# Four spread products of a pair's first expert, moved to a place among its second expert's products

## The chip, the cores and the metric

One Trainium2 chip, one core of it. The metric is the device time of one execution in microseconds (us), taken as the median of the runs. The core has a matrix engine (PE in the profile, with its weight loads listed as PEld), a vector engine (DVE), an activation engine (ACT), GpSimd (POOL), and a queue processor (SP) that here only issues loads. All data is float32; each matrix product stands in the trace as two PE records.

## The reference

Two layers of a diffusion backbone run on two groups of 128 tokens of width 1024 that share one set of weights. Each layer has a token mixer and then a mixture of experts, which is the part that matters here:

```python
def hier_moe(h, w_rg_l, w_re_l, w_e1_l, w_e3_l, w_e2_l):
    x = h.reshape(-1, D_)
    ...
    gate = jnp.einsum('nk,nke->ne', w_top, jax.nn.one_hot(expert_id, N_EXPERTS, dtype=f32))
    hid = jax.nn.silu(jnp.einsum('nd,edf->nef', x, w_e1_l)) * jnp.einsum('nd,edf->nef', x, w_e3_l)
    y = jnp.einsum('nef,efd->nd', hid * gate.astype(x.dtype)[..., None], w_e2_l)
```

There are 16 experts; each token goes to two of them. An expert has three weight matrices: w1 and w3 of 1024 x 512 and w2 of 512 x 1024, 2 MB each.

## The kernel before

A layer first runs its token mixer (a stream of weight chunks against both groups' tokens) and its output projection, router and ranking. Then come the experts, in a pass over all 16 with room for 64 tokens in each; more passes would run only if an expert had more than 64 tokens, and none does here. What is computed for one expert, with `e` its number:

- gather (`gather`, L1021): the tokens routed to the expert are picked out of `h2tok` by products with a 0/1 matrix `e_pick`. One gather serves a pair of experts (64 columns each) and comes in two parts of 8 products. Each part is copied out of PSUM bank XG by DVE (L1723) into `xgT`; the second part waits for the copy of the first, since both use that bank. `e_pick` for the next pair is made by DVE (`pick_pair`, L1709), after it has finished the silu of the pair's second expert.
- two up projections (`up`, L1035), with w1 (`up(0, ...)`) and w3 (`up(1, ...)`), 16 products each. After `up(0)`, ACT and DVE work out the sigmoid and silu (L1310, L1728 to L1730); after `up(1)`, DVE multiplies the two (L1737, `ehid`).
- transposes: of the selection matrix `e_sel` (L1055) and of the hidden values (L1062); ACT copies both out of PSUM (L1318 `e_selT`, L1320 `ehidT`).
- down projection (L1074), 8 products, into PSUM bank OUT; ACT copies it out (L1323, `e_out`).
- spread (`spread_group`, L1042): four products that put the expert's 64 result rows back on the two groups' tokens and add them up in PSUM over all experts.

PE runs experts in pairs (`pair(p, e)`, `i` 0 and 1, eight pairs to a layer) in an order written out by hand. For a pair (a, b) in the middle of the pass it is: up(1) of a; transpose of e_sel; two spreads of the expert before a; transposes of the hidden values; its two other spreads; down of a; up(0) of b; four spreads of a; up(1) of b; gather part 0 for the next pair; transposes of b; gather part 1; down of b; up(0) of the next pair's a. The last pair has no gathers. `n` numbers the expert steps from 1, and each semaphore counts one per step (spread counts four), with one step given in advance.

The weights of the experts come through `ring`, three slots of 2 MB: w1, w3 and w2 of the current expert have one slot each. SP issues the load of a slot for the next expert as soon as PE has finished the last product that reads it; that wait and that issue are all SP does in this stage, in this order and for each expert in turn:

```python
sp.wait_ge(slot_used, used_e(l, p, e, free))
sp.dma_start(ring[:, r, :], dram["stream"][...]).then_inc(slot_loaded[r], 16)
```

For the first expert of a layer w1 and w3 are loaded elsewhere in advance, so its ring slots already hold the second expert's.

Of the kernel before, what the change touches and what calls it, by code (L numbers as in the profile page):

```python
# [36 lines left out]
G = 2  # L37
# [153 lines left out]
def build(nc, dram, out):  # L191
    ctx = ExitStack()
    with ctx:
# [3 lines left out]
        def sem(name):  # L197
            return ctx.enter_context(nc.semaphore(name))
# [126 lines left out]
        def bank(b, n=1):  # L325
            return psum[:, b, :] if n == 1 else psum[:, b:b + n, :]
# [123 lines left out]
        selT_ready = sem("selT_ready")  # L450
# [52 lines left out]
        def ring_e(l, j):  # L503

            return (RING_BASE[l] + FIRST_EXPERT[l] - AHEAD + j) % RING

        def arrived_e(l, p, e, j):

            return p * (NE * 16) + e * 16 + ((RING_BASE[l] + FIRST_EXPERT[l] - AHEAD + j) // RING + 1) * 16

        def step(l, p, e):

            return l * STEPS + p * NE + (e + 1)
# [169 lines left out]
        def _(pe):  # L683
# [68 lines left out]
            for l in range(DEPTH):  # L752
# [150 lines left out]
                for q in ([0, 2, 1, 3] if l == 0 else [0, 1, 2, 3]) + list(range(4, QUARTERS)):  # L903
                    c, g, part = q // 4, (q // 2) % 2, q % 2
# [110 lines left out]
                def gather(n, part, at):  # L1015

                    pe.wait_ge(pick_ready, n + 2)
                    pe.wait_ge(xg_ready, n + part if at == XG else n)
                    for j in range(4):
                        for g in range(G):  # L1020
                            mm = pe.matmul(psum[:, at, j * P:(j + 1) * P], h2tok[:, g, (4 * part + j) * P:(4 * part + j + 1) * P],  # L1021
                                           e_pick[:, g, :], start=(g == 0), stop=(g == G - 1))
                    mm.then_inc(gathered, 1)

                def up(j, p, e, i, ahead=False):

                    if ahead:
                        pe.wait_ge(ahead_loaded[j], l * 16 + 16)
                        w_up = ahead_slot[j].rearrange("p (k n) -> p k n", k=KT)
                    else:  # L1030
                        pe.wait_ge(slot_loaded[ring_e(l, j)], arrived_e(l, p, e + i, j))
                        w_up = ring[:, ring_e(l, j), :].rearrange("p (k n) -> p k n", k=KT)
                    for k in range(KT):
                        for hf in range(2):
                            mm = pe.matmul(psum[halves_of[hf], UP[j], 0:FE // 2], xgT[:, k, halves_of[i]], w_up[:, k, hf * (FE // 2):(hf + 1) * (FE // 2)],  # L1035
                                           start=(k == 0), stop=(k == KT - 1))
                    mm.then_inc(slot_used, 1)

                def spread_group(n, i, g, opens=False, closes=False):

                    for hf in range(2):
                        pe.matmul(bank(Y_MOE[g][hf]), e_selT[i][halves_of[hf], g, :], e_out[halves_of[hf], :], start=opens, stop=closes)\  # L1042
                          .then_inc(spread, 1)

                def pair(p, e, first=False, last=False):
                    for i in range(2):
                        n = step(l, p, e + i)
                        up(1, p, e, i, ahead=first and i == 0 and isinstance(p, int))
                        if i == 1 and not last:
                            gather(n + 1, 0, XG)  # L1050

                        pe.wait_ge(sel_ready, n + 1)
                        pe.wait_ge(eout_ready, n)
                        for g in range(G):
                            mm = pe.transpose(psum[:, OUT, g * P:(g + 1) * P], e_sel[:, g, :], ident)  # L1055
                        mm.then_inc(sel_turned, 1)
                        if i == 0 and not first:
                            pe.wait_ge(selT_ready, n)
                            spread_group(n - 1, 1, 0)
                        pe.wait_ge(hid_ready, n + 1)  # L1060
                        for j in range(2):
                            mm = pe.transpose(psum[:, UP[0], j * P:(j + 1) * P], ehid[:, j * P:(j + 1) * P], ident)  # L1062
                        mm.then_inc(hid_turned, 1)
                        if i == 0 and not first:
                            spread_group(n - 1, 1, 1)
                        if i == 1 and not last:
                            gather(n + 1, 1, XG)

                        pe.wait_ge(hidT_ready, n + 1)
                        pe.wait_ge(selT_ready, n + 1)  # L1070
                        pe.wait_ge(slot_loaded[ring_e(l, 2)], arrived_e(l, p, e + i, 2))
                        for k in range(BT):
                            for hf in range(2):
                                mm = pe.matmul(psum[halves_of[hf], OUT, :], ehidT[:, (k % 2) * P + (k // 2) * CAP:(k % 2) * P + (k // 2) * CAP + CAP],  # L1074
                                               w_down[:, k, hf * W:(hf + 1) * W], start=(k == 0), stop=(k == BT - 1))
                        mm.then_inc(slot_used, 1)
                        if i == 0:
                            up(0, p, e, 1)
                        elif not last:
                            pe.wait_ge(xg_ready, n + 3)  # L1080
                            up(0, p, e + 2, 0)
                        if i == 0 or last:
                            pe.wait_ge(eout_ready, n + 1)
                            for g in range(G):
                                spread_group(n, i, g, opens=first and i == 0, closes=last and i == 1)

                def expert_pass(p):
                    n = step(l, p, 0)
                    pe.wait_ge(eout_ready, n)
                    gather(n, 0, XG)  # L1090
                    gather(n, 1, OUT)
                    pe.wait_ge(xg_ready, n + 2)
                    up(0, p, 0, 0, ahead=isinstance(p, int))
                    pair(p, 0, first=True)
                    with pe.Fori(2, NE - 3, 2) as e:
                        pair(p, e)
                    n_fullest = fullest_expert(pe, l) if isinstance(p, int) else None
                    pair(p, NE - 2, last=True)
                    return n_fullest
# [927 lines left out]
```

## Time and profile before

| | |
|---|---|
| median of 3 runs | 1465.44 us (1465.32 to 1470.59) |
| the profiled execution, its own time | 1467.44 us |
| its span in the profile | 1465.7 us |
| PE busy | 1380.3 us, 94% of the span |
| DVE busy | 520.5 us, 36% |
| ACT busy | 233.9 us, 16% |
| DMA | 259 GB/s over the span, 379.92 MB |

The span is the time from the first to the last instruction of the profile; 1.7 us of the execution lie around it, and the median is 2.0 us under the profiled execution's time. The profile lists, by engine, when each instruction ran, how long the engine sat idle before it, and what released it. The starts of matrix products are exact to some 10 ns and their ends are modelled, so the text below takes times between starts. "x16" behind a row is its number of records, so it is eight products. The experts' stage runs from about 484 to 738 us in layer 0, and from about 1194 to 1447 us in layer 1.

### The profile page before, as it was taken

Reading aid. Unit: us, or ns where it says so; the run is one execution under the profiler, and the core shown is the slowest. Engines: PE = TensorE matmul, PEld = TensorE weight load, DVE = VectorE, ACT = ScalarE, POOL = GpSimd, SP = SyncE. Lnnn points to the kernel's source line nnn. Section 1 sums busy time; section 2 is a strip of 40 time slices with the busy share of each in tenths; the row PEclk is TensorE's granted clock in tenths of the full one; section 3 lists DMA queues with packets and bytes.
Section 4 is the critical chain, followed back from the end, with each engine's and each line's share of the span. In section 5 each row is a group of like instructions: output and inputs, shape, how many; then the busy total and the mean of one; then the engine's idle time right before and its main releaser. Section 6 shows DMA issues by size and latency. Waiting matters only on the chain. (4 is left out here: it accounts for less than half of the span.)

```text
span 1465.7 us, 16950 instructions
## 1 busy us (share of the span) xinstructions
PE 1380.3 (94%) x6662; PEld 723.2 (49%) x6662; DVE 520.5 (36%) x984; ACT 233.9 (16%) x436; POOL 151.1 (10%) x130
## 2 busy tenths in 40 slices
PE   6999989989999999999979999999999999999994
PEld 2445445444445555555534554554444465555551
DVE  1353444422134422323244443452412452322324
ACT  0131220222201011111112122112221111111110
POOL 0123150021200000000001222501120000000000
PEclk9999999999999999999999999999999999999997
DMA  9754544645458299999874445344446628999992
GB/s 384 307 229 157 203 180 143 243 180 223 183 197 331 99 396 396 413 414 412 334 288 174 182 153 200 138 186 186 186 151 234 277 94 332 414 413 397 410 414 113
DMA packets 40263, 379.92 MB, mean 259 GB/s; under 512 B 7946, under 2 KB 12170, under 8 KB 17292
## 3 DMA queue, kind: packets, MB, share of 16 engines
q1 hardware_dynamic: 31776, 375.83, 63.8%
q10 hardware_dynamic: 8428, 3.29, 0.8%
q8 instruction: 39, 0.64, 0.2%
q14 instruction: 20, 0.16, 0.0%
HBM read 374.76 MB, written 4.33 MB: 259 GB/s over the span
## 5 line engine op out<-in xcount | busy, mean ns | idle before, releaser
L926 PE MATMUL psum<-ring,hT 128*128 128x512 f32 x1152 | 520.1, 600 | 13.7 <-DVE rows L1598 8.1
L926 PEld LDWEIGHTS psum<-ring,hT 128*128 128x128 f32 x1152 | 213.8, 192 | 255.1 <-issue 247.5
L1035 PE MATMUL psum<-ring,tbuf 128*64 128x256 f32 x1920 | 216.0, 380 | 1.2 <-DMA ring<-in_stream 1.2
L1035 PEld LDWEIGHTS psum<-ring,tbuf 128*64 128x64 f32 x1920 | 136.0, 137 | 94.2 <-issue 17.5
L1074 PE MATMUL psum<-ring,tbuf 128*64 128x512 f32 x512 | 116.9, 598 | 1.9 <-ACT tbuf L1320 1.9
L1592 DVE TENSOR_TENSOR ch<-psum,bias_ring 128x512 f32<-128x512 f32 x68 | 46.8, 689 | 166.3 <-PE psum L926 166.3
L1728 DVE TENSOR_SCALAR tbuf<-tbuf 128x256 f32<-128x256 f32 x32 | 9.4, 294 | 247.7 <-ACT tbuf L1310 247.7
L950 PE MATMUL psum<-ring,tbuf 128*128 128x512 f32 x192 | 82.9, 593 | 0.0
L1021 PE MATMUL psum<-tbuf,ch 128*128 128x128 f32 x512 | 68.3, 290 | 7.7 <-DVE tbuf L1723 5.0
L1878 POOL TENSOR_SCALAR ldata<-ldata 128x512 f32<-128x512 f32 x24 | 46.1, 1920 | 280.8 <-ACT ldata L1272 269.3
L1021 PEld LDWEIGHTS psum<-tbuf,ch 128*128 128x128 f32 x512 | 62.7, 200 | 16.5 <-issue 9.5
L1827 POOL TENSOR_TENSOR tbuf<-const,sm 128x512 f32<-128x512 f32 x16 | 20.8, 1321 | 480.4 <-DVE sm L1474 453.5
L1042 PE MATMUL psum<-tbuf 64*128 64x512 f32 x256 | 67.4, 626 | 1.4 <-ACT tbuf L1323 1.4
L1074 PEld LDWEIGHTS psum<-ring,tbuf 128*64 128x64 f32 x512 | 33.9, 136 | 70.0 <-issue 59.4
L950 PEld LDWEIGHTS psum<-ring,tbuf 128*128 128x128 f32 x192 | 36.3, 190 | 45.1 <-issue 45.0
L964 PE MATMUL psum<-ring,hT 128*128 128x512 f32 x128 | 55.8, 594 | 1.4 <-ACT hT L1282 1.4
L1729 DVE RECIPROCAL tbuf<-tbuf 128x256 f32<-128x256 f32 x32 | 56.1, 1753 | 1.1
L347 POOL TENSOR_TENSOR hbuf<-hbuf 128x512 f32<-128x512 f32 x28 | 44.0, 1572 | 80.5 <-PE psum L772 80.5
L772 PEld LDWEIGHTS psum<-hbuf 128*128 128x128 f32 x256 | 34.9, 196 | 24.7 <-issue 13.8
L1323 ACT ACTIVATE tbuf<-psum 128x512 f32<-128x512 f32 x32 | 19.1, 597 | 154.6 <-PE psum L1074 154.6
L347 DVE TENSOR_TENSOR hbuf<-hbuf 128x512 f32<-128x512 f32 x28 | 21.6, 770 | 61.9 <-PE psum L772 61.9
L772 PE MATMUL psum<-hbuf 128*128 128x128 f32 x256 | 37.9, 293 | 5.8 <-ACT hbuf L1156 5.6
(269 smaller groups left out, 1153.6 us busy)
## 6 DMA issues: line engine op xcount, KB each, us to landing
ring<-in_stream SPq DMA_DIRECT2D x158, 2048.0 KB, 9.3
ch<-in_stream SPq DMA_DIRECT2D x6, 2048.0 KB, 12.3
bias_ring<-in_b_in SPq DMA_DIRECT2D x36, 256.0 KB, 8.2
ldata<-in_ldata SPq DMA_DIRECT2D x2, 2329.0 KB, 23.7
hbuf<-in_ln SPq DMA_DIRECT2D x4, 1024.0 KB, 11.8
hbuf<-in_stream SPq DMA_DIRECT2D x1, 2048.0 KB, 8.1
tbuf<-in_stream SPq DMA_DIRECT2D x1, 2048.0 KB, 11.6
ch<-in_lb_logits SPq DMA_DIRECT2D x2, 1024.0 KB, 13.4
```

The costliest lines, as they stand in the source:

```text
L347: return engine.tensor_tensor(v, v, other.unsqueeze(3).to_broadcast([P, 2, W // (2 * half), half]), ALU.mult)
L772: mm = pe.matmul(psum[:, PP, hp], (k_x if i else k_sum)[:, hp], crossing(Q_B, Q_F, 1 << (i - 1), hp) if i else q_T[:, hp], start=True, sto ...
L926: mm = pe.matmul(bank(PJ + g), hT[:, k, g * P:(g + 1) * P], w[:, k, :], start=(k == 0), stop=(k == KT - 1))
L950: mm = pe.matmul(bank(BR_BANK[g] + hf), brT[:, b % 2, k, g * P:(g + 1) * P], w[:, k, hf * W:(hf + 1) * W], start=(k == 0), stop=(k == BT - 1))
L964: mm = pe.matmul(bank(2 * hf + g), hT[:, k, g * P:(g + 1) * P], w[:, k, :], start=(k == 0), stop=(k == KT - 1))
L1021: mm = pe.matmul(psum[:, at, j * P:(j + 1) * P], h2tok[:, g, (4 * part + j) * P:(4 * part + j + 1) * P], e_pick[:, g, :], start=(g == 0), ...
L1035: mm = pe.matmul(psum[halves_of[hf], UP[j], 0:FE // 2], xgT[:, k, halves_of[i]], w_up[:, k, hf * (FE // 2):(hf + 1) * (FE // 2)], start=(k ...
L1042: pe.matmul(bank(Y_MOE[g][hf]), e_selT[i][halves_of[hf], g, :], e_out[halves_of[hf], :], start=opens, stop=closes)\
L1074: mm = pe.matmul(psum[halves_of[hf], OUT, :], ehidT[:, (k % 2) * P + (k // 2) * CAP:(k % 2) * P + (k // 2) * CAP + CAP], w_down[:, k, hf * ...
L1592: ins = tt(ch[:, g, c if c < 12 else GATE_BUF[c - 12], :], bank(PJ + g), bias_ring[:, c % RING, :], ALU.add)
L1729: mlink(dve.reciprocal(esig, esig))
L1878: pool.tensor_scalar(sig, sig, 1.0, LN_MAX, ALU.add, ALU.min).then_inc(sig_plus, 1)
```

## The change

The four spread products of the pair's first expert (`i == 0`) no longer stand behind up(0) of the second. They are issued in the second expert's turn, behind its transposes and ahead of gather part 1 (in the last pair: ahead of the down projection, as there is no gather). The products are the same. A wait for `selT_ready` stands before them; the waits for `eout_ready` that covered them are those for the transposes of the same turn. The spreads of each pair's second expert stay where they were, and so do the last pair's four at the very end.

```diff
@@ in pair(p, e, first, last), for i in range(2)
                         mm.then_inc(hid_turned, 1)
                         if i == 0 and not first:
                             spread_group(n - 1, 1, 1)
+                        if i == 1:
+                            pe.wait_ge(selT_ready, n)
+                            for g in range(G):
+                                spread_group(n - 1, 0, g, opens=first)
                         if i == 1 and not last:
                             gather(n + 1, 1, XG)
...
                         elif not last:
                             pe.wait_ge(xg_ready, n + 3)
                             up(0, p, e + 2, 0)
-                        if i == 0 or last:
+                        if i == 1 and last:
                             pe.wait_ge(eout_ready, n + 1)
                             for g in range(G):
-                                spread_group(n, i, g, opens=first and i == 0, closes=last and i == 1)
+                                spread_group(n, 1, g, closes=True)
```

## Rows read from the trace of the kernel before

**Rows 1.** The page's second part: DMA busy tenths in 40 slices of 36.6 us

```profile
DMA  9754544645458299999874445344446628999992
```

**Rows 2.** Windows: us long; busy us (instructions) by engine; clock, DMA share, GB/s

```profile
core 0: us, PE busy (x) PEld busy (x) DVE busy (x) ACT busy (x) POOL busy (x), PEclk, DMA share, GB/s
481.00:485.00 4.00, 2.65 (x18) 2.10 (x17) 1.92 (x12) 0.20 (x1) 0.00 (x0) 1.00 0.00 0
485.00:489.00 4.00, 4.00 (x23) 4.00 (x22) 1.87 (x8) 0.00 (x0) 0.00 (x0) 0.57 0.02 4
656.00:687.00 31.00, 30.65 (x220) 17.15 (x218) 9.02 (x18) 3.39 (x8) 0.00 (x0) 1.00 0.98 410
718.00:719.00 1.00, 0.04 (x2) 0.00 (x0) 0.00 (x0) 0.60 (x1) 0.00 (x0) 1.00 1.03 442
```

**Rows 3.** Timeline of PE, sixth pair of layer 0: start us, length, line, operation, records

```profile
656.43 3.62 PE L1035 MATMUL psum<-ring,tbuf 128*64 128x256 f32 x32
659.98 1.99 PE L1042 MATMUL psum<-tbuf 64*128 64x512 f32 x8
661.90 3.67 PE L1035 MATMUL psum<-ring,tbuf 128*64 128x256 f32 x32
665.50 2.05 PE L1021 MATMUL psum<-tbuf,ch 128*128 128x128 f32 x16
667.39 0.38 PE L1055 MATMUL psum<-const,tbuf 128*128 128x128 f32 x2
667.61 0.38 PE L1062 MATMUL psum<-const,tbuf 128*128 128x128 f32 x2
668.34 2.05 PE L1021 MATMUL psum<-tbuf,ch 128*128 128x128 f32 x16 [0.35 <-DVE tbuf L1723]
670.32 3.65 PE L1074 MATMUL psum<-ring,tbuf 128*64 128x512 f32 x16
673.80 7.08 PE L1035 MATMUL psum<-ring,tbuf 128*64 128x256 f32 x64
...
682.24 0.44 PE L1062 MATMUL psum<-const,tbuf 128*128 128x128 f32 x2
682.61 1.13 PE L1042 MATMUL psum<-tbuf 64*128 64x512 f32 x4
```

**Rows 4.** Timeline of SP's queue: three load issues around that pair

```profile
643.43 0.33 SPq L650 DMA_DIRECT2D ring<-in_stream  x1
...
650.35 0.33 SPq L650 DMA_DIRECT2D ring<-in_stream  x1
...
674.16 0.33 SPq L650 DMA_DIRECT2D ring<-in_stream  x1
```

**Rows 5.** DMA view (last column us to landing), issues at 502.9, 582.0, 643.4, 650.4, 711.8

```profile
ring<-in_stream SPq DMA_DIRECT2D x1, 2048.0 KB, 7.5
...
ring<-in_stream SPq DMA_DIRECT2D x1, 2048.0 KB, 8.1
...
ring<-in_stream SPq DMA_DIRECT2D x1, 2048.0 KB, 7.7
...
ring<-in_stream SPq DMA_DIRECT2D x1, 2048.0 KB, 10.6
...
ring<-in_stream SPq DMA_DIRECT2D x1, 2048.0 KB, 12.1
```

**Rows 6.** Timeline of DVE, same pair

```profile
663.21 0.74 DVE L1709 TENSOR_SCALAR tbuf<-const,tbuf 128x64 f32<-128x64 f32 x4 [0.16 <-DVE tbuf L1730]
...
667.59 0.69 DVE L1723 COPY tbuf<-psum 128x512 f32<-128x512 f32 x1 [1.55 <-PE psum L1021]
```

**Rows 7.** Timeline of PE, last pair of layer 0

```profile
724.54 3.67 PE L1035 MATMUL psum<-ring,tbuf 128*64 128x256 f32 x32
...
728.79 0.44 PE L1062 MATMUL psum<-const,tbuf 128*128 128x128 f32 x2 [0.21 <-SPq L669]
729.70 3.65 PE L1074 MATMUL psum<-ring,tbuf 128*64 128x512 f32 x16 [0.47 <-ACT tbuf L1320]
```

## The prediction

> **What bounds the kernel now.** I read the profile in four steps. First, where the change acts: only in the experts' stage, where the DMA line of the page stands at 9 for slices 15 to 19, counted from 1 [rows 1]. Second, the windows of that stage. In 31 us of it PE is busy 30.65 us at the full clock, and the DMA engines have a share of 0.98 [rows 2]. So two resources look full, and the busy shares can't say which one sets the pace. Third, the timeline of PE through one pair, to see what each product waits for. The only stall it names is 0.35 us in front of gather part 1, waiting for DVE's copy of part 0 [rows 3]. Fourth, the loads. A ring slot is loaded again only when PE has finished with it, so a late product delays a load, and a late load delays a product one expert later. That loop has to be followed through both engines.
>
> The pair of [rows 3] has the period of its neighbours: from the end of one second expert's down projection, seen in the issue of its load at 643.43, to the next at 674.16 is 30.73 us [rows 4]. The load issued at 643.43 finds an empty DMA queue, because the products before it took long and released nothing. It lands 7.7 us later [rows 5]. The two loads issued behind it queue up; the second, w3 for this pair's second expert, is issued at 650.35 and lands 10.6 us later, at 660.95 [rows 4, 5]. That is 17.5 us after the first issue. The up projection that reads it starts at 661.90 [rows 3]. So today the weights are there 0.95 us before they are wanted, and what PE does in between is part of the four spreads that the change takes away from this place.
>
> **What leaves.** The spreads take 661.90 - 659.98 = 1.92 us between the two up projections [rows 3]. Without them up(1) of the second expert could start 3.46 us after up(0) (two up projections back to back have a length of 7.08, one has 3.62 [rows 3]), instead of 5.47 us after. That would be 2.0 us earlier, but the weights land at 660.95, so it starts 0.95 us earlier and PE stands idle for about 1.0 us. The cover that the spreads gave to a load is gone, and half of the time won goes into waiting for it. From a slot's landing to the first product I add 0.05 us, an estimate; its bounds are 0 and 0.3, the latter from the 0.35 us that the gather waits in all for its copy [rows 3].
>
> **What comes.** In the second expert's turn the transposes of the hidden values are now followed by eight PE records of spreads. Before, from that transpose to gather part 1 it took 668.34 - 667.61 = 0.73 us, with the stall for DVE's copy in it. Where a spread follows that transpose today, it takes 682.61 - 682.24 = 0.37 us. So the new stretch is 0.37 + 1.92 = 2.29 us, 1.56 us more than before [rows 3]. The copy that the gather waited for starts at 667.59 and takes 0.69 us [rows 6], so it ends inside the spreads; that stall is gone, and it is the one real gain, about 0.36 us. The added wait for `selT_ready` costs nothing: that copy was made a whole expert earlier, before a down projection that has long finished. Behind it on PE stand the spreads, gather part 1 and the down projection; nobody but they wait on it. The other engines issue the same instructions. ACT's wait for spreads in front of its copy of bank OUT comes after a down projection that itself stands behind the moved spreads. On SP nothing is moved, but each issue follows PE's releases: w1 and w3 for the next pair come earlier, w2, behind the down projection, comes later.
>
> **The sum for a pair in the middle.** I follow the loop from the issue of w2's load (behind the down projection of a second expert) to its next issue: 17.5 us to the landing of w3 [rows 4, 5]; 0.05 to its first product; 3.60 for up(1) (661.90 to 665.50); 1.89 for gather part 0; 0.22 from one transpose to the other; 0.37 + 1.92 for transpose and spreads; 1.98 for gather part 1 (668.34 to 670.32); 3.48 for the down projection (670.32 to 673.80) [rows 3]; 0.36 from there to the issue at 674.16 [rows 4]. That is 31.37 us against 30.73 now: 0.64 us more for a pair. The same view from PE alone: 0.9 us gained at up(1), 1.56 us lost behind the transposes. The time goes into the DMA engines: six loads keep them busy and the seventh, lone one is issued later, so their pause in each pair grows.
>
> **First and last pair.** In a layer's first pair every weight is there in time, but another wait comes next. The gather needs `e_pick`, and DVE finishes it at 663.21 + 0.74 = 663.95, which is 7.52 us after up(0) began at 656.43 [rows 3, 6]. PE would reach the gather 3.46 + 3.60 = 7.06 us after it. So the gather starts 9.07 - 7.52 = 1.55 us earlier than now and the spreads cost 1.56 behind it: nothing is left. In the last pair w3's load, issued at 711.8, lands 12.1 us later, at 723.9; up(1) starts at 724.54 [rows 5, 7], so 0.6 is gained. From the hidden transposes to the down projection it is 729.70 - 728.79 = 0.91 us [rows 7] and will be 2.29, 1.38 more, so 0.75 us lost in sum. A layer has six middle pairs: 6 x 0.64 + 0.75 = 4.6 us. Two layers, and nothing between them that could take it up, since the layer norm and the next layer's work wait for the last spread: 9.2 us. On the profiled execution's 1467.4 us that gives 1476.6. The median of the runs lies 2.0 us below it, so I predict 1474.7 us.
>
> **Bounds.** The uncertain term is the landing of a lone load, on which the two queued ones stand. The lone loads in the stage took 7.5 to 8.1 us, with 7.7 in the pair that I used [rows 5]. The change makes the queue emptier at that point, so I stay with 7.7 and take the ends for the range: from -0.2 to +0.4 us in each of 12 pairs, that is 6.8 to 14.0 us. The forecast's own range is 1472.2 to 1479.4.
>
> **Rivals.** (1) No change. If the lone load landed about 1 us sooner, w3 would be there in time. Then the wait for `e_pick` would be the bound in every pair as in the first, the middle pairs would give nothing, and only the last pair's up(1), 1.9 us earlier against 1.38, would bring 0.5 us in a layer: 1464.4 us. Against it stand all the loads shown, none under 7.5 us [rows 5]; for it, that DMA engines with less to do might serve a lone load sooner. Chance 0.14. The Trainium skill would put us here: its page "DMA: Bandwidth & Descriptors", section "Anatomy of one DMA", gives a fixed 2.0 us plus the bytes over 436 GB/s, an estimate of 6.8 us for such a load, and by it the loop above would be 30.5 us, less than today's 30.73. The trace disagrees by 0.9 us, and the measurement decides.
>
> (2) Faster. The same, and `e_pick` ends 0.47 us sooner because DVE's chain gets shorter. Then PE alone sets the pace and gains 0.44 us in each of 12 pairs and 0.5 in each last one: 1459 us. Nothing in the change shortens that chain of DVE, so 0.04.
>
> (3) Slower by much more. The granted clock falls after PE's idle time: ahead of 485 us PE was busy only 2.65 of 4 us, and in the next 4 us the mean clock was 0.57, nearly all of it at the lower level of 1.2 GHz [rows 2]. Were that to happen behind every new wait, it would cost up to some 1.7 us (half of the 3.4 us that the 0.57 stands for) in 12 pairs, and give about 1495 us. It decides from an idle time longer than the one at 718 us, where PE did nothing for 0.97 us and the clock stayed at 1.00 [rows 2]; the new wait is as long as that one. Chance 0.05.
>
> (4) The spreads don't move in effect, for instance because their stretch is swallowed by another wait in the second expert's turn: 1465.4 us, 0.02; the timeline shows no wait of 1.9 us there.
>
> The same page of the Trainium skill advises, in "Rules for kernel authors", to issue a load early, compute, and wait late. The change does the opposite for w3: it takes computing from ahead of the wait. The trace agrees so far as it shows the landing 0.95 us before the start.
>
> **How the numbers follow.** The forecast has 0.75, rivals (1) to (4) have 0.14, 0.04, 0.05 and 0.02. A measurement of this kernel can tell about 0.5% from no change, which is 7.3 us, so the forecast counts as slower only above 1472.8; its own range reaches just under that, and I put 0.58 of its 0.75 above and 0.17 below. Slower is 0.58 + 0.05 = 0.63; the same is 0.17 + 0.14 + 0.02 = 0.33; faster 0.04. The range takes in rival (1) and the forecast's ends: 1464 to 1479.
>
> **What would show it.** In the changed kernel's timeline up(1) of a middle pair's second expert should have an idle time of about 1 us before it, ended by the DMA of the ring, and start 17.5 us after the lone load's issue. From the transposes to gather part 1 there should be 2.3 us, with no stall for the copy. The period from one lone load to the next should be 31.4 us, the DMA share a little lower, and the gather part 0 should wait for `e_pick` in the first pair alone. A period of 30.7 with a stall at gather part 0 would speak for (1), one of 30.3 for (2), a clock below 1.00 in the stage for (3). The prediction is wrong if lone loads land sooner than 7.5 us, or if the eight records of the moved spreads cost less than 1.9 us in their new place.

## The result, and the profile after

| | before | changed |
|---|---|---|
| median of the runs | 1465.38 us (1464.4 to 1470.59) | 1475.44 us (1471.83 to 1478.86) |
| ratio, 95% interval | | 1.0062 [1.0044, 1.0079] |
| span of the profiled execution | 1465.7 us | 1477.1 us |
| PE busy | 1380.3 us | 1379.1 us |
| mean DMA rate over the span | 259 GB/s | 257 GB/s |
| layer 0's experts | 244.8 us | 248.3 us |
| layer 1's experts | 244.2 us | 249.1 us |

The kernel is slower by 10.1 us in the medians; the forecast was 9.2 (1474.7 us), in a range of 1464 to 1479. The two last lines of the table are worked out from the timeline of PE, from the start of the first up projection of a layer to the start of its last spread record: that is the stretch that the change can alter, called the stage below. They grew by 3.4 and 4.9 us, 8.4 in all. The other 3.0 us by which the two spans differ stand ahead of layer 0's experts, where no instruction differs (the first up projection starts at 493.62 in place of 490.62). So some of the closeness of 10.1 to 9.2 is chance, and the test of the mechanism is in the stages.

The timeline of PE for the sixth pair of layer 0, the pair that [rows 3] shows of before (start us, length, line, records, idle time before it and what ended it):

```profile
661.47 3.62 PE L1035 MATMUL psum<-ring,tbuf 128*64 128x256 f32 x32
666.06 3.67 PE L1035 MATMUL psum<-ring,tbuf 128*64 128x256 f32 x32 [0.96 <-DMA ring<-in_stream]
669.66 2.05 PE L1021 MATMUL psum<-tbuf,ch 128*128 128x128 f32 x16
671.55 0.38 PE L1055 MATMUL psum<-const,tbuf 128*128 128x128 f32 x2
671.77 0.38 PE L1062 MATMUL psum<-const,tbuf 128*128 128x128 f32 x2
672.08 1.99 PE L1042 MATMUL psum<-tbuf 64*128 64x512 f32 x8
674.00 2.05 PE L1021 MATMUL psum<-tbuf,ch 128*128 128x128 f32 x16
675.98 3.65 PE L1078 MATMUL psum<-ring,tbuf 128*64 128x512 f32 x16
679.46 7.08 PE L1035 MATMUL psum<-ring,tbuf 128*64 128x256 f32 x64
```

The spreads have left the place behind the first row, and in their stead stands an idle time of 0.96 us, ended by the DMA of the ring. Behind the transposes the eight records of the spreads stand now, and the 0.35 us stall ahead of gather part 1 is gone.

The queue of SP around that pair, and from the DMA view the time to landing of the first two of these issues:

```profile
648.48 0.33 SPq L650 DMA_DIRECT2D ring<-in_stream  x1
...
655.39 0.33 SPq L650 DMA_DIRECT2D ring<-in_stream  x1
...
679.82 0.33 SPq L650 DMA_DIRECT2D ring<-in_stream  x1
```

```profile
ring<-in_stream SPq DMA_DIRECT2D x1, 2048.0 KB, 7.8
...
ring<-in_stream SPq DMA_DIRECT2D x1, 2048.0 KB, 10.6
```

The lone load (w2's) is issued at 648.48. w3's load is issued at 655.39 and lands 10.6 us later, at 666.0, 17.5 us after the lone load's issue, and up(1) starts at 666.06. From one lone load's issue to the next it is 679.82 - 648.48 = 31.34 us, where before it was 30.73 [rows 4]. The window of a pair, with the fields of [rows 2], and the group of all up projections in layer 0's stage (busy us, mean ns of one | idle us before them, and what ended it):

```profile
656.00:687.00 31.00, 30.04 (x218) 16.88 (x216) 8.69 (x18) 3.08 (x8) 0.00 (x0) 1.00 0.96 401
```

```profile
L1035 PE MATMUL psum<-ring,tbuf 128*64 128x256 f32 x960 | 107.7, 380 | 7.2 <-DMA ring<-in_stream 6.0 <-SPq L669 1.2
```

PE is busy 30.04 us of the 31 where it was busy 30.65, the DMA share is 0.96 for 0.98, the rate 401 GB/s for 410, and the clock is still 1.00 [rows 2]. PE and the DMA engines both looked full, and both have become less full: that is what a longer loop looks like.

### The profile page after: what moved, and what is told of

Its sections match the earlier page's. It is cut to its first block and busy times, and to the rows that moved or that the text cites. A ratio compares the mean times of both kernels' runs of the same rounds, so it can differ in the third digit from the quotient of the medians.

```text
span 1477.1 us, 16950 instructions
## 1 busy us (share of the span) xinstructions
PE 1379.1 (93%) x6662; PEld 721.7 (49%) x6662; DVE 520.3 (35%) x984; ACT 234.0 (16%) x436; POOL 151.1 (10%) x130
## 5 line engine op out<-in xcount | busy, mean ns | idle before, releaser
L926 PEld LDWEIGHTS psum<-ring,hT 128*128 128x128 f32 x1152 | 214.3, 193 | 257.8 <-issue 248.3
L1035 PEld LDWEIGHTS psum<-ring,tbuf 128*64 128x64 f32 x1920 | 136.3, 137 | 102.5 <-DMA ring<-in_stream 24.6
L1727 DVE COPY tbuf<-psum 128x512 f32<-128x512 f32 x32 | 22.1, 691 | 68.5 <-PE psum L1021 68.5
## 6 DMA issues: line engine op xcount, KB each, us to landing
tbuf<-in_stream SPq DMA_DIRECT2D x1, 2048.0 KB, 11.7
```

The source lines that it names most:

```text
L926: mm = pe.matmul(bank(PJ + g), hT[:, k, g * P:(g + 1) * P], w[:, k, :], start=(k == 0), stop=(k == KT - 1))
```

## The experiments

With each version the kernel before ran on the same chip; the times below are medians, the ratios those to the kernel before. Experiments 1 and 2 edit the kernel before, and so does the first half of experiment 3; the others edit the changed kernel. "A pair's period" is the time from one second expert's down projection to the next one's. Two theories were to be told apart. The load loop: the loss arises because w2's load is issued later, and because up(1) can't use the time won, its weights not being there. Its rivals: the new place costs time by itself, whatever the loads do, or PE and DVE alone set the pace.

**1. The old place alone.** The first experts' spreads are left out of the middle pairs.

```diff
                         if i == 0 or last:
                             pe.wait_ge(eout_ready, n + 1)
-                            for g in range(G):
-                                spread_group(n, i, g, opens=first and i == 0, closes=last and i == 1)
+                            if i == 0 and not first and not last:
+                                pe.sem_inc(spread, 2 * G)
+                            else:
+                                for g in range(G):
+                                    spread_group(n, i, g, opens=first and i == 0, closes=last and i == 1)
```

> The kernel before, with the four spreads of a pair's first expert left out of the six middle pairs of each layer (that part of the experts' sum is not computed); first and last pair as before. It tests the half of the sum that says what leaving the old place is worth. Theory of the load loop: up(1) of the second expert can't start before w3 has landed, 17.5 us after the lone load's issue, so only about 0.9 us of the 1.92 are won in a middle pair: period 29.8 us, an idle time of 1.0 us before that up(1) ended by the DMA, and 12 x 0.9 = 11 us in all, about 1454.5 us. Rival, PE and DVE alone set the pace: the next bound is e_pick, 1.5 us are won in each, period 29.2 us, about 1447.5 us.

Measured: 1455.69 us beside 1466.39, ratio 0.9905 [0.9871, 0.9939], 10.7 us less. The timeline of PE in a middle pair:

```profile
628.52 3.62 PE L1035 MATMUL psum<-ring,tbuf 128*64 128x256 f32 x32
632.94 3.67 PE L1035 MATMUL psum<-ring,tbuf 128*64 128x256 f32 x32 [0.80 <-DMA ring<-in_stream]
```

It waits for the DMA, and the period (from the down projection at 611.69 to that at 641.37) is 29.7 us, not 29.2. So of 1.92 us of work taken away 1.0 is won in this pair, and 0.8 in the mean of the twelve (two of them have a period of 30.5 and 31.0 us); the loads hold the rest. The stages are 5.5 and 4.5 us shorter.

**2. The new place alone.** Nothing is taken away; four more products stand where the change puts the spreads.

```diff
+                        if i == 1:
+                            for g in range(G):
+                                for hf in range(2):
+                                    pe.matmul(bank(UP[1]), e_selT[0][halves_of[0], g, :], e_out[halves_of[0], :], start=True, stop=True)
                         if i == 1 and not last:
                             gather(n + 1, 1, XG)
```

> The kernel before, with its spreads where they were, and four products of the same size more (into a PSUM bank whose content is no longer wanted) in the place to which the change moves the spreads, in all pairs. It tests the other half of the sum, what the new place costs. Theory: 2.29 us in place of 0.73 between the transposes and gather part 1, the stall for DVE's copy gone, so 1.56 us more in seven pairs of a layer and 1.38 in the last; the period becomes 32.3 us, PE's own chain being longer then than the load loop, and up(1) of the second expert doesn't wait. About 24.6 us more, 1490 us. Rival, that the new place is cheap because DVE's copy and ACT's copies are waited for anyway: less than 1 us for a pair, under 1480 us.

Measured: 1516.43 us beside 1466.39, ratio 1.0326 [1.0280, 1.0373], twice the loss that I expected. The products themselves were not what I had taken them for:

```profile
582.94 0.38 PE L1062 MATMUL psum<-const,tbuf 128*128 128x128 f32 x2
583.25 3.70 PE L1069 MATMUL psum<-tbuf 64*128 64x512 f32 x8
586.87 2.05 PE L1021 MATMUL psum<-tbuf,ch 128*128 128x128 f32 x16
```

Eight records take 3.70 us here; the eight of the spreads take 1.99 [rows 3]. With 3.62 us from start to start in place of 1.92, the 1.70 us more make 27 us in 16 pairs, and the miss is of that size. The run doesn't measure the new place, so it was made again with two products.

```diff
+                        if i == 1:
+                            for g in range(G):
+                                pe.matmul(bank(UP[1]), e_selT[0][halves_of[0], g, :], e_out[halves_of[0], :], start=True, stop=True)
```

> The run with four extra products measured 3.70 us for them where the four spreads take 1.99: its products all read the first 64 rows, while a spread's two halves read rows 0 to 63 and 64 to 127 and run side by side. So here only two extra products, one after the other, which should take as long as four spreads: a length of about 1.9 us in the new place. Otherwise as before: the kernel before, nothing taken away. Theory: 1.56 us more in seven pairs of a layer and 1.38 in the last, period 32.3 us, 24.6 us in all, about 1491 us. Rival, that part of the extra cost in the run with four was something else than the length of the products: over 1495 us.

Measured: 1486.59 us beside 1466.46, ratio 1.0133 [1.0104, 1.0162]; the two stages are 11.5 and 11.3 us longer, 22.8 in all for 24.6 expected (the medians differ by 20.1). The place costs nearly what was reckoned:

```profile
579.79 0.38 PE L1062 MATMUL psum<-const,tbuf 128*128 128x128 f32 x2
580.10 1.98 PE L1068 MATMUL psum<-tbuf 64*128 64x512 f32 x4
582.01 2.05 PE L1021 MATMUL psum<-tbuf,ch 128*128 128x128 f32 x16
583.99 3.65 PE L1077 MATMUL psum<-ring,tbuf 128*64 128x512 f32 x16
```

From the transposes to gather part 1 it is 582.01 - 579.79 = 2.22 us in place of 0.73, and the period is 32.2 us (583.99 to 616.21). That is 1.5 us more a pair, so the rival that the place is cheap falls. The forecast had 1.56; the difference comes from the step between transposes and products, 0.31 us where I took 0.37. The changed kernel shows the same 0.31.

**3. Short loads.** Both kernels with half of each ring load of the experts. The other half of each slot keeps older values, so the results are others.

```diff
-                    sp.dma_start(ring[:, r, :], dram["stream"][e * 3 + (l * SLOTS + FIRST_EXPERT_SLOT + j)])
+                    sp.dma_start(ring[:, r, 0:SLOT // 2], dram["stream"][e * 3 + (l * SLOTS + FIRST_EXPERT_SLOT + j), :, 0:SLOT // 2])
```

> The kernel before with only half of each ring load of the experts' weights (1 MB in place of 2 MB; the other half of the slot keeps older values, so the experts' results are others). Loads can't set the pace here. Theory: PE's own chain remains, with a period of 30.7 us as before; only the few waits for a slot go, about 1 to 3 us in all, so about 1463 us. Rival, that the loads already set the pace before the change: a period clearly under 30.7 us, and 10 us or more faster.

> The changed kernel with the same half loads. Theory of the load loop: the loss of the change is gone with the loads. up(1) starts right behind up(0), gather part 0 waits about 0.4 us for e_pick, nothing is left over in the middle pairs (period 30.7 us) and the last pair wins 0.6 us, so within 2 us of the kernel before with half loads (1462 us or so). Rival, that the new place costs more whatever the loads do, for instance through the copies of ACT and DVE: 8 to 10 us slower than that kernel, a period of 31.3 us.

Measured: the kernel before with half loads 1462.14 us, ratio 0.9964 [0.9948, 0.9981]; the changed kernel with half loads 1460.32 us, ratio 0.9954 [0.9927, 0.9981]. The stages last 243.6 us (both layers) and 243.2 us. So with loads this short nothing of the change's loss is left; before the change the loads cost only 1.2 and 0.6 us in a stage. The kernel before keeps its period with half loads, so before the change the pace of a middle pair was PE's own chain:

```profile
610.31 3.65 PE L1074 MATMUL psum<-ring,tbuf 128*64 128x512 f32 x16
...
641.03 3.65 PE L1074 MATMUL psum<-ring,tbuf 128*64 128x512 f32 x16
```

That is 30.72 us from start to start. In the changed kernel with half loads the period is 30.80, and the next wait is the one for `e_pick`:

```profile
564.15 7.08 PE L1035 MATMUL psum<-ring,tbuf 128*64 128x256 f32 x64
571.81 2.05 PE L1021 MATMUL psum<-tbuf,ch 128*128 128x128 f32 x16 [0.58 <-DVE tbuf L1713]
```

**4. Only the lone load shortened**, in the changed kernel.

```diff
-                    sp.dma_start(ring[:, r, :], dram["stream"][e * 3 + (...)]).then_inc(slot_loaded[r], 16)
+                    if j == 2:
+                        sp.dma_start(ring[:, r, 0:SLOT // 2], dram["stream"][e * 3 + (...), :, 0:SLOT // 2]).then_inc(slot_loaded[r], 16)
+                    else:
+                        sp.dma_start(ring[:, r, :], dram["stream"][e * 3 + (...)]).then_inc(slot_loaded[r], 16)
```

> The changed kernel, with only the w2 loads halved (1 MB; the other half of that slot keeps older values, so the down projections compute with wrong weights there); w1 and w3 are loaded whole. In a middle pair the lone load is that of w2, and w1 and w3 queue behind it. Theory: the lone load lands 2.4 us sooner, w3 some 15.1 us after its issue in place of 17.5, no wait before up(1), the period is 30.7 us and the whole loss is gone: about 1464 us, within 3 us of the kernel before. Rival, that w3's own load or its late issue is what up(1) waits for: nothing but w2 changes, the wait stays near 1 us, and the time stays near 1475 us.

Measured: 1463.73 us beside 1466.46, ratio 0.9976 [0.9957, 0.9994]; the stages last 245.1 and 244.4 us, 0.3 and 0.2 more than in the kernel before, where the changed kernel had 3.4 and 4.9 more. The DMA view for the issues at 615.8 (w2), 619.3 (w1) and 622.7 (w3):

```profile
ring<-in_stream SPq DMA_DIRECT2D x1, 1024.0 KB, 5.0
...
ring<-in_stream SPq DMA_DIRECT2D x1, 2048.0 KB, 7.7
...
ring<-in_stream SPq DMA_DIRECT2D x1, 2048.0 KB, 9.2
```

w3 lands at 622.74 + 9.2 = 631.9, 16.1 us after w2's issue. I had said 15.1: w1's load is issued 1.6 us before the short one lands, nothing else is queued, and it takes 7.7 us again. up(1) starts at 632.27 behind up(0) without a wait. Halving a load that up(1) never reads takes its wait away: the queue is the link between w2's issue and w3's landing.

**5. The second wait.** Half loads again, and `e_pick` made ahead of the silu.

```diff
                             select(n + 1, e + 1)
-                            silu(n + 1)
                             if not last:
                                 pick_pair(n + 2, e + 2)
+                            silu(n + 1)
```

> The changed kernel with half loads as in the earlier run (half of each ring load of the experts, so other results), and on DVE the next pair's e_pick is made ahead of the silu, in DVE's idle time, not behind it. It tests the second wait that I named: without loads, the gather waits for e_pick. Theory: that wait of 0.5 to 0.6 us goes in seven pairs of a layer, the period of a middle pair falls from 30.7 to 30.2 us, and the stages become 3.5 us shorter each than in the run with half loads alone: about 1453.5 us. Rival, that something else holds part 0 of the gather: period 30.7, no difference.

Measured: 1453.38 us, ratio 0.9914 [0.9885, 0.9942]; both stages last 238.9 us, 4.3 less than without the DVE edit. The gather starts right behind up(1):

```profile
594.65 7.08 PE L1035 MATMUL psum<-ring,tbuf 128*64 128x256 f32 x64
601.66 2.05 PE L1021 MATMUL psum<-tbuf,ch 128*128 128x128 f32 x16
```

A pair's period is 30.15 us. So the order that the change makes would win if loads and `e_pick` left room: the wait for the DVE copy that it removes is followed by two others, first the one for the ring and behind it the one for `e_pick`.

**6. The changed kernel again**, on the chip of the next version.

> The changed kernel as it is, on the same chip as the split version. Theory: 8.4 to 9.2 us more than the kernel before, ratio about 1.006, with 8.4 us of it in the two experts' stages. Rival, that part of the measured difference was elsewhere in the kernel: the stages 8.4 us longer but the ratio under 1.004.

Measured: 1474.13 us beside 1466.46, ratio 1.0048 [1.0029, 1.0066]. The stages last 250.4 and 249.3 us, 10.7 more than before in sum; with the 8.4 of the first profile that brackets the 9.2 worked out ahead. Of the 10.7, 1.9 stand in one pair of layer 0 with a period of 33.2 us. All these differences go back to one profile of the kernel before.

**7. Half of the spreads moved.**

```diff
                         if i == 1:
                             pe.wait_ge(selT_ready, n)
-                            for g in range(G):
-                                spread_group(n - 1, 0, g, opens=first)
+                            spread_group(n - 1, 0, 1, opens=first)
...
+                        if i == 0:
+                            pe.wait_ge(eout_ready, n + 1)
+                            spread_group(n, 0, 0, opens=first)
                         if i == 1 and last:
```

> A version made from what the runs say: of the four spreads of a pair's first expert two (group 0) stay between the two up projections, two (group 1) move behind the transposes. Theory: up(1) starts 0.86 us earlier, about when w3 has landed, so nothing is waited away; behind the transposes stand 0.37 + 1.06 = 1.43 us in place of 0.73, and the stall for DVE's copy is gone. PE's chain is 30.57 us and the load loop 30.5 us: 0.16 us less in seven pairs of a layer, 0.34 in the last, 3 us in all, ratio to the kernel before about 0.998. Rival, that any spread behind the transposes costs more than it saves: slower than before, ratio 1.003, halfway to the changed kernel.

> The split version once more, beside the one with the down projection first. Theory: ratio 0.998 to the kernel before, as in its first run (0.9974), 2 to 4 us slower than the other. Rival: no difference between the two.

Measured: 1462.18 us beside 1466.46, ratio 0.9974 [0.9960, 0.9987], and the second time 1462.37 beside 1465.11, 0.9980 [0.9968, 0.9993]. Against the changed kernel on the same chip it is 12 us faster. It beats the kernel before by 4.3 us and the second time by 2.7, a quarter of a per cent, with the stages 1.8 and 1.0 us shorter than before:

```profile
624.88 3.62 PE L1035 MATMUL psum<-ring,tbuf 128*64 128x256 f32 x32
628.43 1.13 PE L1042 MATMUL psum<-tbuf 64*128 64x512 f32 x4
629.50 3.67 PE L1035 MATMUL psum<-ring,tbuf 128*64 128x256 f32 x32
633.11 2.05 PE L1021 MATMUL psum<-tbuf,ch 128*128 128x128 f32 x16
635.00 0.38 PE L1055 MATMUL psum<-const,tbuf 128*128 128x128 f32 x2
635.21 0.38 PE L1062 MATMUL psum<-const,tbuf 128*128 128x128 f32 x2
635.52 1.13 PE L1042 MATMUL psum<-tbuf 64*128 64x512 f32 x4
636.58 2.05 PE L1021 MATMUL psum<-tbuf,ch 128*128 128x128 f32 x16
```

No row has an idle time. Two products between the up projections cover w3's landing, two behind the transposes cover DVE's copy.

**8. The down projection ahead of gather part 1.** The loop says that w2's load should be issued sooner.

```diff
                         if i == 1:
                             pe.wait_ge(selT_ready, n)
-                            for g in range(G):
-                                spread_group(n - 1, 0, g, opens=first)
-                        if i == 1 and not last:
-                            gather(n + 1, 1, XG)
+                            spread_group(n - 1, 0, 0, opens=first)
+                            if last:
+                                spread_group(n - 1, 0, 1)
...
                         elif not last:
+                            gather(n + 1, 1, XG)
+                            spread_group(n - 1, 0, 1, opens=first)
                             pe.wait_ge(xg_ready, n + 3)
                             up(0, p, e + 2, 0)
```

(`e_pick` is made ahead of the silu as above.)

> A version that follows from the loop: what stands between w3's landing and the down projection delays w2's load, so it is moved behind the down projection. The first expert's spreads: group 0 behind the transposes, group 1 behind gather part 1; gather part 1 itself comes after the down projection of the second expert (last pair: all four spreads ahead of the down projection); e_pick is made ahead of the silu. Theory: the load loop becomes 28.5 us and binds no more, the six loads need 29.3 us, and PE's chain is 30.3 us: 0.4 us less than the kernel before in seven pairs of a layer and 0.6 in the last, 6.8 us in all, ratio 0.995 to 0.996. Rival, that the second part's copy now stands in front of the next up(0): a wait of some 0.5 us there, no gain over the split version (0.9974).

Measured: 1473.63 us beside 1465.11, ratio 1.0058 [1.0033, 1.0082]: slower, and neither the theory nor the rival foresaw that. PE waits for the ring in the group of the up projections, and the window from 520 to 720 us and the DMA queue in it (packets, MB, share of the 16 engines) show engines nearly as busy as in the half-moved version, and moving less. This version first, the half-moved one second:

```profile
L1035 PE MATMUL psum<-ring,tbuf 128*64 128x256 f32 x960 | 107.8, 381 | 7.6 <-DMA ring<-in_stream 6.8 <-SPq L669 0.8
...
520.00:720.00 200.00, 192.35 (x1366) 105.61 (x1362) 56.23 (x112) 21.32 (x50) 0.00 (x0) 1.00 0.97 390
...
q1 hardware_dynamic: 5362, 77.96, 96.7%
```

```profile
520.00:720.00 200.00, 199.25 (x1414) 109.88 (x1412) 57.52 (x114) 22.66 (x53) 0.00 (x0) 1.00 0.98 409
...
q1 hardware_dynamic: 5610, 81.82, 98.4%
```

The packets themselves take longer: one of 16 KB 0.65 us in the mean where it takes 0.63 in the half-moved version, and 10% of them over 0.68 us where it is 3%. A busy share counts such a packet as busy for all of its time.

The same version with half of each ring load:

> The version with the down projection ahead of gather part 1, with half of each ring load of the experts (so other results). With whole loads it came out 2 periods of about 32 us long, where I had worked out 30.3, and PE waited for the ring. This run tells whether its PE chain was reckoned wrong or its loads. Theory: the chain was right, so with half loads the period is 30.3 us, the stages 5.5 us each shorter than in the kernel before, about 1453 us. Rival, the new order has a wait of its own on PE, DVE or ACT: a period over 31 us with half loads too, over 1460 us.

Measured: 1457.27 us beside 1465.78, ratio 0.9952 [0.9916, 0.9989]; the stages last 241.3 us, 3.5 and 2.8 less than before, for 5.5 expected. The timeline of PE shows a stretch of one pair in this order:

```profile
599.43 2.05 PE L1021 MATMUL psum<-tbuf,ch 128*128 128x128 f32 x16
601.32 0.38 PE L1055 MATMUL psum<-const,tbuf 128*128 128x128 f32 x2
601.54 0.38 PE L1062 MATMUL psum<-const,tbuf 128*128 128x128 f32 x2
601.85 1.13 PE L1042 MATMUL psum<-tbuf 64*128 64x512 f32 x4
602.91 3.65 PE L1077 MATMUL psum<-ring,tbuf 128*64 128x512 f32 x16
606.50 2.05 PE L1021 MATMUL psum<-tbuf,ch 128*128 128x128 f32 x16
608.48 1.13 PE L1042 MATMUL psum<-tbuf 64*128 64x512 f32 x4
609.54 7.13 PE L1035 MATMUL psum<-ring,tbuf 128*64 128x256 f32 x64
```

There is no wait in it. The period is 30.5 us, so the PE chain of that order was reckoned some 0.2 us too short, which is the smaller part. What makes the version slow is in the loads: it is gone with half of their bytes. Why packets take longer when whole loads are issued in that order stays open; I have no run that tells it.

## Why the prediction was right

- **What bounds the kernel.** That a loop through SP's queue sets the pace once the spreads are gone was the core of it, and runs 3 and 4 show it by removing bytes. Before the change the loop had 0.95 us to spare in the pair shown, and PE's chain of 30.72 us set the pace; the busy shares alone could not have told that.
- **One reading was wrong, and cost nothing.** The prediction says that the lone load at 643.43 finds an empty queue. It doesn't: the load before it lands only at 645.0, 1.6 us after that issue (after the change 0.9 us after it). Nothing is queued behind that load, so the engines still run dry while the new load starts: their mean busy share is 0.2 from 644.0 to 644.5 us before, and 0.02 from 648.75 to 649.25 after. From its landing to the lone load's it is 6.1 us before and 6.9 after, where the queued loads land 4.9 us apart. So the loads lose 1.2 us in this pair before the change and 2.0 after it. The sum is untouched, because it took the 17.5 us from the issue to w3's landing as measured. The range of 7.5 to 8.1 us for lone loads also leaves out the one of layer 0's last pair, which took 9.2; the forecast doesn't use it, as the last pair was worked out from w3's own landing.
- **What leaves.** Forecast: up(1) 0.95 us earlier and an idle time of about 1.0 us. Measured: up(1) starts 4.59 us after up(0) (666.06 less 661.47) for 5.47 before, 0.88 earlier, with 0.96 us of idle time, and from the lone load's issue to up(1) it is 17.58 us for 17.55. Run 1, which does this half alone, won 0.8 us a pair (9.8 us in 12 by their periods).
- **What comes.** Forecast 1.56 us; measured 2.23 - 0.73 = 1.50 in the changed kernel. The step from the transposes to the spreads was the mis-sized term, 0.31 for 0.37. Run 2 in its second form does this half alone.
- **The middle pairs.** 31.34 us in the pair shown for a forecast of 31.37, both against 30.73. Over all twelve the periods run from 31.1 to 32.0 us and the mean is 0.60 more than before, for 0.64 forecast.
- **First pair.** Forecast: nothing, because the gather waits for `e_pick`. From the first up projection of the layer to the down projection of the second expert it is 26.05 us before and 25.88 after, so a little is won. The gather does wait for `e_pick` there, 0.38 us, and in no middle pair. With half loads (run 3) it waits in every middle pair too, 0.58 us, and run 5 takes that away.
- **Last pair.** Forecast 0.75 us lost. From the seventh pair's second down projection to the eighth's it was 28.66 us (729.70 less 701.04) and is 29.05 in layer 0; in layer 1 it was 27.91 and is 29.14. So 0.4 and 1.2 were lost, 0.8 in the mean; neither layer alone bears the 0.75 out. The 2.29 us between the hidden transposes and the down projection came as forecast:

```profile
724.71 3.67 PE L1035 MATMUL psum<-ring,tbuf 128*64 128x256 f32 x32 [0.61 <-DMA ring<-in_stream]
729.60 3.67 PE L1035 MATMUL psum<-ring,tbuf 128*64 128x256 f32 x32 [1.22 <-SPq L669]
...
733.85 0.44 PE L1062 MATMUL psum<-const,tbuf 128*128 128x128 f32 x2 [0.21 <-DVE tbuf L1741]
734.22 1.99 PE L1042 MATMUL psum<-tbuf 64*128 64x512 f32 x8
736.14 3.65 PE L1078 MATMUL psum<-ring,tbuf 128*64 128x512 f32 x16
```

  What the forecast left out is the wait of up(0) for w1: 0.61 us now in both layers, 0.97 before in layer 0 and 0.23 in layer 1. The 1.22 us ahead of up(1) end with w3's landing at 729.55, though the view names SP's queue.
- **The sum.** 4.6 us a layer forecast; 3.4 and 4.9 in the first profile, 5.6 and 5.1 in the second. The parts of the first profile are 7.2 us in the middle pairs, 1.6 in the last ones and 0.4 won in the first ones.
- **The rivals.** (1), no change, needed a lone load about 1 us shorter. The run with short w2 loads made w3 land 1.4 us sooner, and the time was that of no change within 3 us; so the mechanism was sound and its condition false: lone loads took 7.5 to 7.9 us in all pairs but the last, and about 9 there. The Trainium skill's formula ("DMA: Bandwidth & Descriptors", "Anatomy of one DMA"), an estimate of 6.8 us for such a load, would have chosen it. The page gives that fit for DMAs issued from GpSimd, while these are issued from SP, so the prediction carried it further than the page does. The lone load of the pair shown took 7.8 us and doesn't agree with 6.8, which says nothing on the fit for the page's own path. (2) needed `e_pick` sooner as well: run 5 is that case, 11.7 us faster than the kernel before, 5 us more than the 6 I had worked out; its half loads also take the waits of the last pairs away, so it isn't that rival alone. (3), the clock: 1.00 in the window shown, with a new wait in it. (4), no effect: the stages grew.

## What to carry to other kernels

When a buffer is loaded again as soon as its reader is done, work that stands between two products can be the cover of a load; follow the loop issue, landing, product, release through both engines before moving it. Here 1.92 us of products were worth only 0.8 to 1.0 us ahead of a wait that ends late, and cost 1.5 us between a load's landing and the release that issues the next one. Where one block of small products has to cover two short waits, splitting it may serve both, as in run 7.

## What the runs showed of the hardware

- Spread products of 64 rows whose two halves sit in rows 0 to 63 and 64 to 127 take 1.99 us for eight records; eight records of that size all in rows 0 to 63 take 3.70 (run 2). That fits two halves running side by side. It isn't shown to be the rows alone, because the products of run 2 also all write one PSUM bank, where a spread's halves write two.
- A lone load of 2 MB takes 7.5 to 8.1 us from issue to landing (8.8 to 9.2 in three of the four last pairs of the two kernels), one of 1 MB 4.9 to 5.7 (run 4), while loads that queue behind another mostly land 4.9 us after it. So a lone load costs almost 3 us more than a queued one if nothing is moving at its issue. If it is issued 1.6 us before the load ahead of it lands, as in the kernel before, 1.2 us of that are lost in the pair shown; at 0.9 us, as in the changed kernel, 2.0 us are.
- Nearly the same DMA share can hide different rates: 409 GB/s at 0.98 and 390 GB/s at 0.97, with mean packets of 0.63 and 0.65 us. The rate, not the share, tells whether loads are delivered.
- Runs of one and the same kernel differ by more than this change is worth: the kernel before ran from 1461.3 to 1473.4 us. In the profiles the experts' stages agree to a few tenths where the loads don't bind (243.0 to 243.2 us in the two profiles of run 7), and part of the difference lies elsewhere (the first up projection starts at 490.6 us in one profile and 495.5 in another). Where the loads bind, the stage scatters too: layer 0's was 248.3 and 250.4 us in the two profiles of the changed kernel. For changes of this size the length of the stage in the trace tells more than a single total.
